# Seven products in place of eight in the down projections of a macaron decoder layer

## The reference, cut to what matters

```python
def swiglu(h, w_in, w_out):
    gu = h @ w_in
    g, u = jnp.split(gu, 2, axis=-1)
    return (jax.nn.silu(g) * u) @ w_out
...
    x = x + 0.5 * rmsnorm(swiglu(h, ffn1_w_in, ffn1_w_out), ffn1_norm_post)
    ... attention and gated mix ...
    x = x + 0.5 * rmsnorm(swiglu(h, ffn2_w_in, ffn2_w_out), ffn2_norm_post)
```

## Time and profile before

| | us |
|---|---|
| median of 3 runs (2030.86 to 2032.71) | 2031.97 |
| the profiled execution | 2032.04 |
| its span | 2030.2 |

### The profile page before, as it was taken

The page is one execution under the profiler, slowest core; times in us unless marked ns, Lnnn a source line. Parts: engine busy times, 40 slices in busy tenths (PEclk is TensorE's granted clock), DMA queues, the critical chain, the costliest instruction groups (busy, mean ns, idle before and its releaser), DMA issues.

```text
span 2030.2 us, 23559 instructions
## 1 busy us (share of the span) xinstructions
PE 2002.1 (99%) x9154; PEld 1660.9 (82%) x9154; DVE 1351.5 (67%) x1514; ACT 1044.7 (51%) x1342; POOL 86.3 (4%) x144
## 2 busy tenths in 40 slices
PE   8999999999999999999999999999999999999997
PEld 6888888888888878888888888878888888988886
DVE  6788888756555474456655665588888886565554
ACT  6555555445444454445555554465555654544442
POOL 0000000001000000000100000000100001000000
PEclk9999999999999999999999999999999999999999
DMA  6777777766555655554454556557776778575553
GB/s 237 234 245 231 243 232 230 247 217 240 192 184 175 220 166 187 179 191 157 158 165 146 166 189 209 181 166 238 227 249 224 242 239 259 182 246 199 195 185 107
DMA packets 206440, 415.26 MB, mean 205 GB/s; under 512 B 9169, under 2 KB 17666, under 8 KB 205826
## 3 DMA queue, kind: packets, MB, share of 16 engines
q1 hardware_dynamic: 198610, 388.16, 57.5%
q0 software_dynamic: 7264, 22.55, 4.2%
q10 hardware_dynamic: 464, 3.15, 0.4%
HBM read 400.46 MB, written 13.37 MB: 204 GB/s over the span
## 4 chain that ended last, share of the span: by engine, by line
PE 93%; DVE 2%; ACT 2%; DMA 2%; issue 1%; POOL 0%; DVEq 0%; ACTq 0%; POOLq 0%
PE acc L552 16%; PE acc L554 16%; PE acc L553 16%; PE acc L629 11%; PE acc L631 11%; PE acc L630 11%; PE tp L631 3%; PE tp L629 3%; PE tp L630 3%; PE tp L579 1%; DVE w_lo L1186 1%; PE tp L793 1%; DMA blocks<-short_bounce 1%; PE tp L767 1%; ACT w_hi L880 1%
## 5 line engine op out<-in xcount | busy, mean ns | idle before, releaser
L1186 DVE TENSOR_TENSOR w_lo<-raw,w_hi 128x1024 fp32r<-128x1024 f32 x408 | 497.8, 1225 | 449.6 <-ACT w_hi L880 446.3
L880 ACT ACTIVATE w_hi<-raw 128x1024 fp32r<-128x1024 f32 x408 | 428.6, 1058 | 433.3 <-PE acc L554 429.1
L902 ACT ACTIVATE w_hi<-raw 128x1024 fp32r<-128x1024 f32 (+1 forms) x400 | 404.8, 1023 | 327.8 <-PE acc L631 225.5
L1219 DVE TENSOR_TENSOR w_lo<-raw,w_hi 128x1024 fp32r<-128x1024 f32 (+1 forms) x400 | 465.2, 1178 | 152.2 <-ACT w_hi L902 150.0
L629 PE MATMUL acc<-w_hi,h_hi 128*128 128x512 f32 (+1 forms) x928 | 354.6, 382 | 0.6 <-DVE w_lo L1219 0.6
L630 PE MATMUL acc<-w_lo,h_hi 128*128 128x512 f32 (+1 forms) x928 | 354.3, 382 | 0.0
L631 PE MATMUL acc<-w_hi,h_lo 128*128 128x512 f32 (+1 forms) x928 | 354.3, 382 | 0.0
L552 PE MATMUL acc<-w_hi,h_hi 128*128 128x512 f32 x736 | 294.1, 400 | 8.3 <-DVE w_lo L1186 6.5
L554 PE MATMUL acc<-w_hi,h_lo 128*128 128x512 f32 x736 | 288.3, 392 | 0.0
L553 PE MATMUL acc<-w_lo,h_hi 128*128 128x512 f32 x736 | 287.6, 391 | 0.0
L552 PE MATMUL acc<-w_hi,a_hi 128*128 128x512 f32 x688 | 268.2, 390 | 3.1 <-DVE w_lo L1186 3.1
(11 more groups left out here) (151 smaller groups left out, 1789.4 us busy)
## 6 DMA issues: line engine op xcount, KB each, us to landing
raw<-in_ffn_w_in SPq DMA_DIRECT2D x126, 1024.0 KB, 5.2
raw<-in_w_in SPq DMA_DIRECT2D x68, 1024.0 KB, 5.2
raw<-in_ffn_w_out SPq DMA_DIRECT2D x56, 1024.0 KB, 5.1
raw<-in_ffn_w_in SPq DMA_DIRECT2D x68, 512.0 KB, 4.5
raw<-in_ffn_w_out SPq DMA_DIRECT2D x40, 768.0 KB, 4.3
raw<-in_w_out SPq DMA_DIRECT2D x16, 1024.0 KB, 5.1
raw<-in_ffn_w_in SPq DMA_DIRECT2D x16, 768.0 KB, 4.5
bounce<-blocks POOLq DMA_DIRECT2D x20, 512.0 KB, 3.7
```

Of the source, the lines that this page charges most:

```text
L880: nc.scalar.activation(w_hi[:, s % 4], raw[:, g % 4, s % 2 * 2:s % 2 * 2 + 2], ACT.Copy)\
L902: nc.scalar.activation(w_hi[:, s % 4, 0:n], raw[:, g % 4, s % 2 * 2:s % 2 * 2 + n], ACT.Copy)\
L1186: nc.vector.tensor_tensor(w_lo[:, s % 4], raw[:, g % 4, s % 2 * 2:s % 2 * 2 + 2], w_hi[:, s % 4].bitcast(F32), ALU.subtract).then_inc(lo_r ...
L1219: nc.vector.tensor_tensor(w_lo[:, s % 4, 0:n], raw[:, g % 4, s % 2 * 2:s % 2 * 2 + n], w_hi[:, s % 4, 0:n].bitcast(F32), ALU.subtract).the ...
```

## The change

The down stages B and H take the first 16 K tiles as eight *sets* of two K tiles by two adjacent output columns (a column pair) by two row tiles. A set has eight block products; it now takes seven, of sums of blocks (the Winograd form). Set s uses K tiles 2s and 2s + 1. The remaining 27 K tiles are ordinary. The columns go in two column pairs (t = 0, 1), each 60 subs long; both columns of a pair collect at the same time in `acc[:, 0]` and `acc[:, 1]`, and the partial products that belong to several outputs collect in four `tp` banks.

Subs of one column pair: 0 to 5 ordinary; set 0 in subs 6 to 9; then one ordinary place (two subs) between each two sets: 10, 11; set 1 in 12 to 15; 16, 17; set 2 in 18 to 21; and so on to set 7 in 48 to 51; 52 to 59 ordinary. A set fills two ring places: the first holds the four loaded blocks (two DMAs of 512 KB), of which DVE makes three sums into the second and one into the first. Its subs have 2, 2, 2 and 1 block products; an ordinary sub has 4.

The activation sums (`set_raw`, `set_hi`, `set_lo`) are made by `make_sets` and `round_sets` in four groups of two sets, groups 0 and 1 in the gate sides of pairs 9 and 10, groups 2 and 3 in steps 14 to 30 of the first column pair. They lie where `xs` and `h` were, so x is read again from DRAM (`x_again`) in the second column pair, from a copy `x_held` in stage H, which is written at the start of stage F. The hook for the last three K tiles moves from steps 7 and 8 to steps 12 and 13. At a column's end DVE adds the PSUM bank to the partial sums in SBUF (`add`), and ACT squares that sum in SBUF.

```diff
+    return (std((0, 4), (0, 5), (1, 4)) + both() + std((1, 5)) + both() + std((0, 6)) + both() + std((1, 6))
+            + both() + std((0, 7)) + both() + std((1, 7)) + both() + std((0, 8)) + both() + std((1, 8)) + both()
+            + std((0, 9), (0, 10), (1, 9), (1, 10)))
...
+                def set_raws(j, s, t):
+                    sp.wait_ge(lo_ready, 2 * j - 6)
+                    src = w[2 * s * P:(2 * s + 2) * P, 2 * t * CW:(2 * t + 2) * CW]
+                    src = src.rearrange("(two p) (c n) -> p two c n", p=P, c=2)
+                    sp.dma_start(raw[:, j % 4, 0:4:3, :], src[:, 1]).then_inc(raw_in[j % 4], 16)
+
+                    sp.wait_ge(raw_in[(j + 1) % 4], 16 * ((j + 1) // 4))
+                    sp.dma_start(raw[:, j % 4, 1:3, :], src[:, 0]).then_inc(raw_in[(j + 1) % 4], 16)
...
+            def x_again(b8, f, src):
+
+                for m in range(MT):
+                    done = set_at(2 * m + 1, SET_SUMS) + 2
+                    gp.wait_ge(multiplied, 8 * b8 + DOWN_LEN + done)
+                    gp.dma_start(xs[:, m, :], src[:, m, :]).then_inc(x_back, 16)
+                    gp.wait_ge(x_back, 16 * (MT * f + m + 1))
...
                 elif n == R_PRE[2]:
+                    gp.wait_ge(x_new, 2 * len(UPDATES))
+                    gp.dma_start(x_held, xs[:]).then_inc(x_saved, 16)
                     move_blocks(1)
+                    x_again(H8, 1, x_held)
...
+                    kind, arg, half = DOWN_SUBS[r]
+                    if kind == STD:
+                        par, k, tiles = arg
+                        return [(par, m, from_a(k + 2 * half + i, m), i) for m in range(MT)
+                                for i in range(down_blocks(r))]
+                    if kind == SET_RAW and half == 0:
+                        return [(0, 0, from_a(2 * arg + 1, 0), 0), (2, 0, from_a(2 * arg, 0), 1)]
+                    if kind == SET_RAW:
+                        return [(0, 1, from_a(2 * arg + 1, 1), 0), (1, 0, from_set(3, arg), 1)]
+                    if half == 0:
+                        return [(2, 1, from_set(0, arg), 0), (2, 2, from_set(2, arg), 1)]
+                    return [(2, 3, from_set(1, arg), 0)]
...
+                g = s // 2
+                kind, arg, half = down_kind(p + LEAD)
+                if s % 2 == 0:
+                    act.wait_ge(raw_in[g % 4], 16 * (g // 4 + 1))
+                if kind == SET_RAW and half == 0:
+                    act.wait_ge(raw_in[(g + 1) % 4], 16 * ((g + 1) // 4 + 1))
+                elif kind in (SET_RAW, SET_SUMS):
+                    act.wait_ge(set_sums, DOWN_SETS * (2 * f + (p + LEAD) // DOWN_LEN) + arg + 1)
+                act.wait_ge(multiplied, s - 3)
+                n = down_blocks(p + LEAD)
...
+            def round_sets(f, g):
+                act.wait_ge(set_joined, DOWN_GROUPS * f + g + 1)
+                nc.scalar.activation(set_hi[g][:], set_raw[g][:], ACT.Copy).then_inc(set_hi_ready, 1)
...
+                end = DOWN_LEN - SKEW
+                hooks = {12: lambda: round_a(f, PAIRS), 16: lambda: round_sets(f, 2), 28: lambda: round_sets(f, 3),
...
+                def join():
+                    dve.wait_ge(a_ready, 2 * ((PAIRS + 1) * f + g + 1))
+                    if g < 2:
+                        dve.wait_ge(stage_ready, 2 * fast_count(f, PAIRS))
+                        if f:
+                            dve.wait_ge(x_saved, 16)
+                    for m in range(MT):
+                        v = slice(m * P, (m + 1) * P)
+                        ins = nc.vector.tensor_tensor(joined[g // 2][m][:], a_hi[:, 4 * g:4 * g + 4, v].bitcast(F32),
+                                                      a_lo[:, 4 * g:4 * g + 4, v].bitcast(F32), ALU.add)
+                    link(ins)
+
+                def sums():
+                    even, odd = [[joined[g // 2][m][:, i:4:2, :] for m in range(MT)] for i in range(2)]
+                    c = set_raw[g]
+                    nc.vector.tensor_tensor(c[:, 2], even[0], even[1], ALU.subtract)
+                    link(nc.vector.tensor_tensor(c[:, 0], even[1], odd[1], ALU.add))
+                    link(nc.vector.tensor_tensor(c[:, 1], c[:, 0], even[0], ALU.subtract))
+                    nc.vector.tensor_tensor(c[:, 3], odd[0], c[:, 1], ALU.subtract).then_inc(set_joined, 1)
+
+                def rest():
+                    dve.wait_ge(set_hi_ready, DOWN_GROUPS * f + g + 1)
+                    nc.vector.tensor_tensor(set_lo[g][:], set_raw[g][:], set_hi[g][:].bitcast(F32),
+                                            ALU.subtract).then_inc(set_ready, 1)
+                return {1: join, 2: sums, 4: rest}
...
+            def down_split(b8, f, p):
+                s = 8 * b8 + p + LEAD
+                kind, arg, half = down_kind(p + LEAD + 1)
+                if kind == SET_RAW and half == 0:
+                    g = (s + 1) // 2
+                    x, v = raw[:, g % 4], raw[:, (g + 1) % 4]
+                    dve.wait_ge(raw_in[g % 4], 16 * (g // 4 + 1))
+                    dve.wait_ge(raw_in[(g + 1) % 4], 16 * ((g + 1) // 4 + 1))
+
+                    dve.wait_ge(lo_ready, 2 * g - 4)
+                    link(nc.vector.tensor_tensor(v[:, 0:2, :], x[:, 2:4, :], x[:, 1:3, :], ALU.subtract))
+                    link(nc.vector.tensor_tensor(v[:, 2, :], x[:, 3, :], v[:, 0, :], ALU.subtract))
+                    nc.vector.tensor_tensor(x[:, 2, :], x[:, 0, :], v[:, 2, :], ALU.subtract).then_inc(set_sums, 1)
...
+                def add(n, m):
+                    dve.wait_ge(partial_out, 2 * f + n // 2 + 1)
+                    nc.vector.tensor_tensor(part(n, m), part(n, m), acc[:, n % 2, m, :],
+                                            ALU.add).then_inc(acc_free[n % 2], 1)
...
+                hooks = {13: lambda: rest_of_a(f, PAIRS), 14: join, 15: sets[2], 18: sets[4], 25: more[1], 26: more[2], 30: more[4],
+                         SHARED_END + 1: a0, SHARED_END + 2: b0, end: lambda: both(0, end),
+                         end + 2: lambda: (scale_y(0, 0), scale_y(0, 1)),
+                         n8: lambda: both(1, n8), n8 + 2: lambda: (scale_y(1, 0), scale_y(1, 1)),
+                         n8 + SHARED_END + 1: a1, n8 + SHARED_END + 2: b1, n8 + end: lambda: both(2, n8 + end)}
...
+                def first_row():
+                    scale_y(2, 0)
+                    scale_y(2, 1)
+                    dve.wait_ge(tile0_done, (1, 3, 4)[k])
+                    add(3, 0)
+                    post_var(0)
+                    scale_y(3, 0)
...
+                at = n8 + end + 1
+                if k == 2:
+                    hooks[at] = lambda: (first_row(), update(0, 1, 2, 3))
+                else:
+                    scale, lo = pieces_of(PC_PRE[k + 1], SKIP_PRE[k + 1], PIECES, pre_gain(k + 1))
+                    hooks[at] = lambda: (first_row(), update(0, 1))
+                    hooks[at + 1] = lambda: (scale(0, 1), update(4, 6), lo(0))
...
+                if k == 2:
+                    dve.wait_ge(multiplied, 8 * b8 + 2 * n8)
+                    add(3, 1)
+                    post_var(1)
+                scale_y(3, 1)
+                update(*((4, 5, 6, 7) if k == 2 else (2, 3)))
```

More of the change, by code:

```diff
@@ L93, in fast_count, with down_slots, both, std @@
     return len(FAST_PAIRS) * k + len([f for f in FAST_PAIRS if f < i])
+DOWN_GROUPS = 4
+DOWN_SETS = 2 * DOWN_GROUPS
+SET_RAW, SET_SUMS = range(4, 6)
+def down_slots():
+    s = iter(range(DOWN_SETS))
+    def both():
+        n = next(s)
+        return [(SET_RAW, n), (SET_SUMS, n)]
+    def std(*parts):
+        return [(STD, (par, 4 * i, min(4, FT - 4 * i))) for par, i in parts]
+    return (std((0, 4), (0, 5), (1, 4)) + both() + std((1, 5)) + both() + std((0, 6)) + both() + std((1, 6))
+            + both() + std((0, 7)) + both() + std((1, 7)) + both() + std((0, 8)) + both() + std((1, 8)) + both()
+            + std((0, 9), (0, 10), (1, 9), (1, 10)))
+DOWN_SLOTS = down_slots()
+DOWN_LEN = 2 * len(DOWN_SLOTS)
+DOWN_SUBS = [(kind, arg, half) for kind, arg in DOWN_SLOTS for half in range(2)]
+DOWN_SUBS += DOWN_SUBS
+assert len(DOWN_SUBS) % 8 == 0
+DOWN8 = len(DOWN_SUBS) // 8
+SHARED_END = 2 * DOWN_SLOTS.index((SET_SUMS, DOWN_SETS - 1)) + 2
+def down_kind(r):
+    return DOWN_SUBS[r] if r < len(DOWN_SUBS) else (STD, (0, 0, 4), r % 2)
+def down_blocks(r):
+    kind, arg, half = down_kind(r)
+    if kind == STD:
+        return min(2, arg[2] - 2 * half)
+    return 1 if kind == SET_SUMS and half else 2
+def set_at(s, kind):
+    return 2 * DOWN_SLOTS.index((kind, s))
 A8 = 0
 B8 = A8 + FFN8
-C8 = B8 + NG * 3
+C8 = B8 + DOWN8
 G8 = C8 + QKV_CHUNKS
@@ L103 @@
 H8 = F8 + FFN8
-TOTAL_SUBS = 8 * (H8 + NG * 3)
+TOTAL_SUBS = 8 * (H8 + DOWN8)
 PC_START = 0
@@ L164, in chunk_hooks @@
     return {j: (lambda fs=hooks[8 * g + j]: [f() for f in fs]) for j in range(8) if 8 * g + j in hooks}
-def out_subs():
-    subs, k = [], 0
-    for n in OUT_GROUPS:
-        subs += [list(range(k, k + 2)), list(range(k + 2, k + n))]
```

(8 more changed lines are left out.)

181 lines of the change are left out of this document (160 added, 21 removed).

## The result

The changed kernel took 2034.19 us (median of 20 runs), the kernel before 2030.32 us (20 runs beside them): ratio 1.0018, with a 95% interval of 1.0011 to 1.0025. It is slower by 3.9 us, where 3 us less were forecast. The profiled executions have spans of 2034.0 and 2030.2 us; what follows divides up these 3.8 us. Neither is a median one: that of the changed kernel is the slowest of its 20 (2036.03 us), that of the kernel before took 2032.04.

The account below looks back on a forecast made before the run. TensorE, busy 2002.1 of 2030.2 us, was taken to bound the kernel. The terms -21.8 - 3.6 + 7.8 + 10.6 + 2.8 + 1.2 gave -3.0 from 2032.04, so 2029.0 us, with a range of 2020 to 2038.

Parts of the forecast that it names:

- 1 matmuls: Down stages B and H: 32 block products fewer, 96 matmuls at 0.2267 us each, -21.8 us.
- 2 moved hook: Near the start of B and H: TensorE no longer stands still for the last tiles, -3.6 us for both.
- 3 weight sums between the splits: Ordinary places between sets: TensorE waits 0.17 plus 0.11 us for DVE at each of 28, +7.8 us.
- 4 activation sums: First column pairs of B and H: sums in DVE's tight stretch delay splits, 5.3 us per stage, +10.6 us.
- rival B: Sets' loads land late beside reads of x, 2.0 us each for four reads, giving 2037 us; chance 0.10.
- 5 from B to C: Boundary from B to C: DVE's adds and later reduction delay TensorE, with less work to hide it, +2.8 us.
- 6 end of H: End of H: DVE is free only after TensorE, then adds, and ACT squares, +1.2 us.
- Rival A: Hand-overs fit, so the wait between sets is absent and the kernel is faster, about 2021 us; chance 0.17.
- Hidden, with 1.6 to spare: Transfers in the down stages: a set's loads land in 5.1 us where 6.7 are left, so they cost nothing.
- the signs: Expected in the profile: some 28 to 36 TensorE waits for DVE of 0.1 to 2 us, 14 to 15 in all.

Follow-up runs that it names:

- experiment 5: Kernel before, last tiles' rounding and subtractions in B and H moved three subs later, nothing else changed: 2028.28 us against 2029.71, ratio 0.9992.
- Experiment 1: Changed kernel with VectorE's weight sums of a set one sub later, ahead of the split of the set's own first sub: 2017.10 us, ratio to before 0.9938.
- experiment 4: Changed kernel with the second column pair's reads of x all behind the last set's loads: 2032.28 us, ratio to the kernel before 1.0012.
- experiment 2: Changed kernel with the third and fourth groups' activation sums, joins and roundings moved to steps 0 to 5: 2026.91 us, ratio to the kernel before 0.9987.

## Why the prediction was wrong

Each term against the two profiled executions. Where a stage's part can't be read singly, it is the rest: stage B, from its first matmul to the first transposes of C's `stage`, is 5.8 us longer (475.1 to 746.16 before, to 751.94 after); with 10.9 of matmuls and 2.5 of hook gone and 3.2 more at the boundary, its waits and its halved clock are 16.0 us. H likewise: 11.6. Together 27.6.

| step | predicted | measured | from |
|---|---|---|---|
| 1 matmuls | -21.8 | -21.8 | 96 rows fewer |
| 2 moved hook | -3.6 | -3.6; -1.4 in the medians | no wait there; experiment 5 |
| 3 weight sums between the splits | +7.8 | +9.5 | 28 x 0.34 |
| 4 activation sums | +10.6 | +10.7 | stalls in front of subs 17 to 29, beyond the regular waits |
| x read back (rival B) | 0 | +3.0 | 1.62 + 2 x 0.68 beyond the regular wait |
| halved clock | none | +3.4 | starts in two stretches |
| in no stall | none | +1.0 | 27.6 less 9.5, 10.7, 3.0, 3.4 |
| 5 from B to C | +2.8 | +3.2 | gaps 6.9 against 3.7 |
| 6 end of H | +1.2 | +1.8 | 6.8 against 4.9 |
| closing of the program | none | -3.4 | 3.1 against 6.5 |
| sum | -3.0 | +3.8 | spans |

The mechanisms of steps 3 to 6 were right. Step 4 came within 0.1 us; steps 3, 5 and 6 are 0.4 to 1.7 us each too small, and 1.0 us stands in no stall. Experiment 1 shows step 3's: it is the place of the sums, between two splits that TensorE needs, that costs. In step 3 the wait is 0.23 + 0.11 and not 0.17 + 0.11; the value rested on a difference of 0.17 in 6.29. The first part of step 4 was read almost exactly for H: in H the stalls are 1.56, 0.61, 0.42 and 0.78 where 1.50, 0.73, 0.35 and 0.91 were forecast. In B the first is 2.05: DVE's operations there are longer (1.58 for the join that takes 1.29 elsewhere) while GpSimd builds its distances beside them; no run separates the two.

Rival A went with the rule of the Trainium skill's page "VectorE: DVE Perf Modes" (The DRAIN you can't avoid) that a semaphore after each operation costs nothing. The trace disagrees again: from 534.07 to 534.80 are 0.73 us between two operations of 512 of which the second awaits the first, and 0.61 from 534.80 to 535.41, where VectorE's next operation does not.

**What failed** is the step "Hidden, with 1.6 to spare" of the transfers, and the clock, which the sum put at nothing without a word. The step took 5.1 us for a set's loads with or without a read beside them. The late loads in B landed up to 8.0 us after their issue, and from the first issue (631.25) to the landing (639.62) are 8.4 us where 6.7 were left. Rival B stood in the text with its mechanism; three landings were late (by 1.63 us at most, not 2.0), and experiment 4 shows that the reads cause it. No term held the clock, though step 4 itself forecast a wait of 1.50 us and the signs named waits of up to 2; experiment 2 shows that without the long stalls it stays whole. These two are 6.4 us and by themselves change the sign. The sizes that were too small, with what stands in no stall, are 3.8 more; the closing hid 3.4 of it by luck. Last, the forecast was made against 2032.04 us, and the kernel before has a median of 2030.3: its hook wait was near the longest in the first profile, so 1.7 us of the baseline and some 2 of step 2's 3.6 were one draw. The changed kernel's profile is a draw too, 1.8 us above its median: how much of the 3.0 and the 3.4 a median execution has, no run shows.

Right were: no wait at the start of B and H, the 28 regular waits and their place, the longest stalls in front of subs 17 and 29 of the first column pairs, and that it is decided at the ring's ordinary places between sets, by DVE's order there.

## What to carry to other kernels

When a step takes matmuls out and gives VectorE work for it, count VectorE's work between two operations that TensorE waits for, not over the stage; put work that is wanted late behind the splits that are wanted soon. Here that one move of three operations by one sub turned 3.9 us of loss into 12.5 of gain, and with the activation sums moved to loose steps 17. A wait that hangs on a landing differs from run to run: read it in several profiles before it stands in a sum. And a stall of 2 us can cost more than 2: half clock behind it added 1.6 to 1.8.
